# Four projection chunks of block one by seven block products, and another order of products in the first such chunk of block two

## The reference, cut to what matters

```python
hn = rms_norm(x, g_mix[l])
proj = hn @ w_in[l]
(qa, ka, va, ra, alr, qb, kb, vb, qi, ki, wi, gate_a, gate_b) = jnp.split(proj, split_points, axis=-1)
ya = gla_mixer(qa, ka, va, ra, alr, ...) @ w_br_gla[l]
yb = dsa_mixer(qb, kb, vb, qi, ki, wi, rel_bias) @ w_br_att[l]
mixed = jax.nn.sigmoid(gate_a) * ya + jax.nn.sigmoid(gate_b) * yb
x = x + mixed @ w_out[l]
x = x + hier_moe(rms_norm(x, g_ffn[l]), ...)
```

## Time and profile before

| | us |
|---|---|
| median of 3 runs | 933.66 (933.52 to 935.08) |
| the profiled execution, its own time | 934.74 |
| its span in the profile | 932.9 |

### The profile page before, as it was taken

The page is one execution under the profiler, slowest core; times in us unless marked ns, Lnnn a source line. Parts: engine busy times, 40 slices in busy tenths (PEclk is TensorE's granted clock), DMA queues, the critical chain, the costliest instruction groups (busy, mean ns, idle before and its releaser), DMA issues.

```text
span 932.9 us, 21571 instructions
## 1 busy us (share of the span) xinstructions
PE 792.4 (85%) x9619; PEld 578.7 (62%) x9619; DVE 260.1 (28%) x648; ACT 196.7 (21%) x415; POOL 71.1 (8%) x76
## 2 busy tenths in 40 slices
PE   7999999999999999999999888757676675756754
PEld 4565688884676657876757676646464464545643
DVE  2142930232422247684435111101001010010101
ACT  2112222331321133426525011101010020100100
POOL 6200300000001130190000000000000000000000
PEclk9999999999999999999999999988788899897988
DMA  9995624059899999444577999999999999999995
GB/s 304 329 330 183 245 93 179 1 197 420 325 396 416 402 364 331 162 174 163 225 268 298 422 430 424 426 427 427 427 428 431 429 430 428 428 429 427 428 428 229
DMA packets 55558, 310.18 MB, mean 332 GB/s; under 512 B 5426, under 2 KB 7178, under 8 KB 43088
## 3 DMA queue, kind: packets, MB, share of 16 engines
q1 hardware_dynamic: 50848, 301.60, 80.6%
q0 software_dynamic: 2912, 4.37, 1.6%
q10 hardware_dynamic: 1744, 3.41, 1.0%
HBM read 307.76 MB, written 4.19 MB: 334 GB/s over the span
## 4 chain that ended last, share of the span: by engine, by line
PE 62%; DMA 33%; issue 2%; DVE 2%; ACT 1%; DVEq 0%; SPq 0%; ACTq 0%
PE ps L1863 59%; DMA ring<-in_w_up 22%; DMA ring<-in_w_down 5%; DMA ring<-in_w_gate 5%; PE ps L1889 1%; PE ps L2191 1%; PE ps L2044 1%; DMA xx<-in_x 0%; PE ps L1903 0%; PE ps L2234 0%; PE ps L1920 0%; PE ps L2006 0%; ACT arena L845 0%; PE ps L2084 0%; PE ps L1911 0%
## 5 line engine op out<-in xcount | busy, mean ns | idle before, releaser
L1863 PE MATMUL ps<-ring,arena 128*32 128x128 f32 (+2 forms) x4912 | 228.9, 319 | 93.9 <-DMA ring<-in_w_gate 44.0
L1863 PEld LDWEIGHTS ps<-ring,arena 128*32 128x32 f32 (+1 forms) x4912 | 178.9, 126 | 142.6 <-DMA ring<-in_w_gate 52.8
L1863 PE MATMUL ps<-arena 32*128 32x256 f32 (+9 forms) x1412 | 143.3, 365 | 1.6 <-ACT arena L929 0.9
L1863 PEld LDWEIGHTS ps<-arena 32*128 32x128 f32 (+4 forms) x1412 | 96.3, 168 | 35.2 <-issue 27.9
L1863 PE MATMUL ps<-ring,xx 128*128 128x512 f32 (+2 forms) x344 | 114.4, 486 | 0.6 <-issue 0.6
L1863 PEld LDWEIGHTS ps<-ring,xx 128*128 128x128 f32 x344 | 64.2, 190 | 41.7 <-issue 34.9
L1863 PE MATMUL ps<-ring,const 128*32 128x256 f32 x864 | 58.8, 413 | 25.4 <-DMA ring<-in_w_down 22.4
L1863 PE MATMUL ps<-xx,ring 128*128 128x256 f32 x288 | 64.9, 382 | 0.0
L1863 PEld LDWEIGHTS ps<-ring,const 128*32 128x32 f32 x864 | 28.1, 116 | 52.2 <-issue 34.0
L1863 PEld LDWEIGHTS ps<-xx,ring 128*128 128x128 f32 x288 | 53.8, 190 | 8.0 <-issue 0.7
L918 ACT ACTIVATE g_dil<-ps 128x128 f32<-128x128 f32 x16 | 4.4, 277 | 189.0 <-PE ps L1863 189.0
(11 more groups left out here) (331 smaller groups left out, 713.0 us busy)
## 6 DMA issues: line engine op xcount, KB each, us to landing
ring<-in_w_up SPq DMA_DIRECT2D x37, 2048.0 KB, 25.1
ring<-in_w_gate SPq DMA_DIRECT2D x36, 2048.0 KB, 23.6
ring<-in_w_down SPq DMA_DIRECT2D x32, 2048.0 KB, 23.9
ring<-in_w_in SPq DMA_DIRECT2D x15, 2048.0 KB, 20.1
arena<-in_w_down SPq DMA_DIRECT2D x6, 2048.0 KB, 9.9
ring<-in_w_out SPq DMA_DIRECT2D x4, 2048.0 KB, 7.9
arena<-in_w_gate SPq DMA_DIRECT2D x4, 2048.0 KB, 16.0
arena<-in_w_up SPq DMA_DIRECT2D x2, 2048.0 KB, 17.4
```

Source lines behind the costliest of these rows:

```text
L1863: ins = pe.matmul(dst, w, x, start=start, stop=stop, skip_group_check=True)
```

## The change

- `chunk` and `tm_chunk` are replaced by one function `seven(c, s, q, block, between)` that does a chunk by seven products in an order given by `PRODUCTS[c]`. Chunks 0 to 3 are now kb, vb, va and ra of block one; the five of block two are chunks 4 to 8. `between` names what is done ahead of which product.
- The four chunks of block one share one pair of weight-sum buffers (at 80 of the arena) and their own buffers for the token sums (at 50). So the first weight sum of one chunk waits until the fourth product of the chunk before it is done. In block two there are two pairs, as before.
- ACT evicts five times in each of the four chunks (128 x 256), where it evicted once (128 x 512); DVE adds three times (128 x 256), where it evicted once, and makes four weight sums of 128 x 1024 each.
- The exponential of the GLA gate and its logarithm now stand inside the evictions of va, behind the transfer of the bias row, which stood behind them. The decays stand inside the evictions of ra. SiLU is no longer applied on the way out of PSUM: it is done in SBUF once all parts of ra are added.
- The second selection of DVE is cut in two: four rounds, then the addition and the weight sum of ra, then four rounds and the mask.
- In the first chunk of block two product 5 comes ahead of 6 and 3 ahead of 7; the forget logits move from behind product 1 to ahead of product 4 (the last), and ACT's absolute value and exponential of them, and what follows, into the next chunk. The forget sums move from between the second and third chunk into the third, ahead of product 7. DVE has the scale factors ahead of the second token sum.

```diff
-        t_sum = [[kb3(at + 4 * i, 4, T) for i in range(2)] for at in (62, 74)]
-        a_sum = [kb3(82 + 2 * i, 4, P) for i in range(4)]
+        t_sum = [[kb3(at + 4 * i, 4, T) for i in range(2)] for at in 4 * (80,) + (62, 74, 62, 74, 62)]
+        a_sum = [[kb3(at + 2 * i, 4, P) for i in range(4)] for at in (50, 82)]
...
-        SUM_BANKS = [(0, 1, 2), (3, 6, 7)]
+        SUM_BANKS = [(0, 1, 2), (3, 0, 1), (2, 3, 0), (1, 0, 3)] + 2 * [(0, 1, 2), (3, 6, 7)] + [(0, 1, 2)]
+        PRODUCTS = [(1, 2, 6, 5, 7, 3, 4)] * 4 + [(1, 2, 5, 6, 3, 7, 4)] + [(1, 2, 6, 5, 7, 3, 4)] * 4
...
+            chunk(0, k_tm, ahead=index_queries)
+            index_relu(0)
+            chunk(1, v_tm)
+            index_relu(1)
...
+            chunk(2, va, ahead=gate_exp, behind=gate_ln)
+            chunk(3, ra, behind=decays)
+            act.wait_ge(s_sev, 4 * N7 + 1)
+            act.wait_ge(s_pev_d, 7)
+            act.activation(ra, ra, ACT.Silu).then_inc(s_pev_a, 1)
...
                 if j == 1:
                     dve.wait_ge(s_slot[s % RING], turn_value(dve, 16 * (s // RING + 1), q, 16))
-                    if c >= 2:
+                    if 1 <= c < N7:
+                        dve.wait_ge(s_prod, 7 * (c - 1) + 4)
+                    elif c >= N7 + 2:
                         dve.wait_ge(s_prod, 7 * (c - 2) + 4)
...
-            select(1)
+            select(1, range(4))
+            add_second(ra, 3)
+            weight_sum(3, 4, 0)
+            select(1, range(4, TOPK // 8))
+            add_part(ra, 3)
+            add_third(ra, 3)
...
+            def seven(c, s, q, block, between={}):
+                arrived(s, q)
...
+                factors = {1: (bx, xnT[:, low, 0:P], w[:, low, left], True, False),
+                           2: (by, xnT[:, high, 0:P], w[:, high, left], True, True),
+                           3: (bz, s4, w[:, high, right], False, True),
+                           4: (bx, xnT[:, high, P:T], w[:, high, left], False, True),
+                           5: (bz, s1, t1, True, False),
+                           6: (bx, s2, t2, False, False),
+                           7: (bx, s3, w[:, low, right], False, False)}
+                for p in PRODUCTS[c]:
+                    b, x, w4, start, stop = factors[p]
+                    if p in between:
+                        between[p]()
+                    if p in (3, 4, 6, 7):
+                        pe.wait_ge(s_sev, act_out(c, {6: 1, 7: 6, 3: 5, 4: 7}[p]))
+                    if p in (3, 5, 6, 7):
+                        pe.wait_ge(s_asum, 4 * block + {5: 1, 6: 2, 7: 3, 3: 4}[p])
+                    if p in (4, 5, 6, 7):
+                        pe.wait_ge(s_tsum, 4 * c + {5: 1, 6: 2, 7: 3, 4: 4}[p])
+                    for k in range(4):
+                        ins = mm(bank(b, T), x[:, k, :], w4[:, k, :], start and k == 0, stop and k == 3)
+                    ins.then_inc(s_prod, 1)
...
+            seven(0, CH_KB, 0, 0, {1: lambda: evicted(1, 1), 6: index_transposes})
+            index_scores(0)
+            seven(1, CH_VB, 0, 0, {2: lambda: evicted(3, 3)})
+            index_scores(1)
...
+            seven(2, CH_VA, 0, 0, {5: lambda: evicted(5, 5)})
+            seven(3, CH_RA, 0, 0, {2: lambda: evicted(6, 6), 7: decay_sums})
...
+            block2_chunk(0, {5: lambda: pe.wait_ge(s_fpe, 1), 4: forget_logits})
+            block2_chunk(1)
+            block2_chunk(2, {7: forget_sums})
```

More of the change, by code:

```diff
@@ L891, in norm_by_tile, with out_of_psum, head_squares, chunk @@
                         act.dma_start(xs_dram[tt * P:(tt + 1) * P, :], xs[:, tt, :]).then_inc(s_xd, 16)
+            def out_of_psum(dst, c, p, b, tt):
+                act.wait_ge(s_prod, product_done(c, p))
+                if c < N7:
+                    return act.activation(dst, bank(b, T), ACT.Copy)
+                return act.activation(dst, bank(b, T), ACT.Copy, scale=x_rstd[:, tt:tt + 1])
+            def head_squares(x, i, evicted):
+                act.wait_ge(s_pev_a, CH_BG + evicted)
+                act.wait_ge(s_pev_d, 7 + evicted)
+                act.activation(kb(12 + 4 * i, 1024), x, ACT.Square).then_inc(s_sq, 1)
+            def chunk(c, dst, ahead=None, middle=None, behind=None):
+                bx, _, bz = SUM_BANKS[c]
+                out_of_psum(dst[:, 0, 0:T], c, 1, bx, 0).then_inc(s_sev, 1)
+                if ahead:
+                    ahead()
+                for p in ACT_OUTS[c][1:]:
+                    if p == 5:
+                        out_of_psum(c22_part[c], c, 5, bz, 1).then_inc(s_sev, 1)
+                    else:
+                        tt = int(p == 7)
+                        out_of_psum(dst[:, tt, T:2 * T], c, p, bx, tt).then_inc(s_sev, 1)
+                    if p == 6 and middle:
+                        middle()
+                if behind:
+                    behind()
+                last = out_of_psum(dst[:, 1, 0:T], c, 4, bx, 1)
+                last.then_inc(s_sev if c == 3 else s_pev_a, 1)
             def sparse_attention():
@@ L1043, in _ @@
             act.wait_ge(s_rs, FACTORS["x2"])
[L1045 to L1067, removed]
             def forget_abs_exp():
@@ L1612, in _ @@
             dve.tensor_scalar(q_tm[:, 1, :], bank(3), x_rstd[:, 1:2], None, ALU.mult).then_inc(s_pev_d, 1)
+            dve.wait_ge(s_xs, 2)
+            for j in range(1, 5):
+                x_sum(j, 0)
+            weight_sums(0, 0)
             dve.wait_ge(s_proj, 2)
@@ L1766, in _ @@
                                          op1=ALU.add).then_inc(s_fl, 1)
[L1767 to L1773 removed]
+            add_second(k2_tm, 5)
+            weight_sum(5, 4, q1)
+            weight_sums(6, q1)
             dve.wait_ge(s_fl, F_LN)
@@ L1951, in normed @@
                 pe.wait_ge((s_nev_a, s_nev_d)[k // 2 % 2], NEV0[m] + 2 * (k // 4) + k % 2 + 1)
-            def tm_chunk(w, b0, between=None):
-                for tt in range(TT):
-                    if tt == 1 and between:
-                        between()
-                    for k in range(KD):
-                        ins = mm(bank(b0 + tt), xnT[:, k, tt * P:(tt + 1) * P], w[:, k, :], k == 0, k == KD - 1)
-                ins.then_inc(s_proj, 1)
-                read[0] += 1
             def free_pair(n, base_a, base_d, last_d):
```

306 lines of the change are left out of this document (143 added, 163 removed).

## The result

| | before | after |
|---|---|---|
| median of six runs, us | 934.75 (933.52 to 937.64) | 929.69 (929.45 to 933.49) |
| ratio | | 0.9946, interval 0.9930 to 0.9962 |
| the profiled execution / its span | 934.74 / 932.9 | 933.49 / 931.7 |

The change makes the kernel 5.06 us faster. 7.0 was forecast, and the range ended at 929.6. Two things make up the distance between 926.7 and 929.69: the gain is 1.94 too small, and the kernel before, with three more runs, stands at 934.75 and not at 933.66, which is the other 1.09. The profiled execution of after happens to be its slowest, 3.8 above the median. TensorE also starts 0.68 later in it than in the kernel before.

What follows compares the result with a forecast made beforehand. It took TensorE's work up to about 500, then a fixed amount of bytes, as the bound. 7.4 - 2.3 + 1.9 = 7.0 off the median 933.66 gave 926.7, range 923.8 to 929.6.

Steps and rivals of the forecast that it cites:

- What bounds the kernel: Whole kernel: TensorE work up to about 500, then fixed bytes; a microsecond off TensorE before 500 moves the end by one.
- rival (e): Tail from slice 23 on moves fewer bytes a microsecond; gain gone from 1.6%, 936 at 2.2%; chance 0.04.
- Part 1: Block one's four chunks kb, vb, va, ra by seven products: 1.85 us saved in each, 7.4 off.
- rival (d): New waits for the chunks' evictions and sums, 0.35 for each of 20, eat the gain: 933.7; chance 0.05.
- Part 2: GLA behind ra: POOL's addition holds up DVE by the shared lock, so TensorE waits for `kdec`, 2.3 us back.
- rival (b): GLA: bias lands after 97.5, POOL's two additions run across `kdec`; wait 4.7, time 929.1; chance 0.12.
- Rival (a): GLA behind ra: no new wait, the lock between POOL and DVE is passed by; time 924.4; chance 0.16.
- Part 3: First chunk of block two: waits, 1.35 of them for ACT, go away; 1.9 us off, bounds 0.5 and 2.5.

## Why the prediction was wrong

- **What bounds the kernel: right.** What TensorE won ahead of 500 arrived at the end: 4.9 at the load for `xx`, 5.1 in the medians. The tail's rate is the same in the changed kernel (rival (e) is out for it), though with 32 one-element products a loss came there by another way.
- **Part 1, 7.4: the term was mis-sized; it is 6.51.** Two steps failed, this one (0.89) and the one that the prediction left out, told last (1.25). Here it took as the price of the old chunk less that of the new one 13.93 - 12.08 = 1.85, four times. It took 12.08 from the middle of a row of like chunks, from one start to another with products of the same kind on both sides, and 13.93 from a chunk that begins and ends beside other shapes. Like for like: va and the first tile of ra of before, 48 records, take 99.15 - 78.45 = 20.70 (view below), and the 16 of the second tile 107.87 - 100.83 = 7.04, so 32 in the middle cost 13.66 and the true difference there is 1.58; with both ends it is 1.64, as vb showed. Nothing of the 0.89 is a wait that the rows show: DVE's weight sums and ACT's evictions are hidden, as forecast, and rival (d) is out.

```profile
78.45 20.87 PE L1863 MATMUL ps<-ring,xx 128*128 128x512 f32 x48
...
100.83 7.11 PE L1863 MATMUL ps<-ring,xx 128*128 128x512 f32 x16
```

- **Part 2, 2.3 back: 1.91 (1.51 when run again); the mechanism is right, its timing was not, and that the sizes are near is luck.** The bias went out at 75.96, as worked out, but POOL could ask for it only at 90.17, 14.2 later, where it was 9.8 before (timelines of ACT and POOL below). It landed after 97.5, the case of rival (b); but (b) let both additions run behind each other across `kdec`. In fact `kdec` got in between them, and so waited for 2.1 us of the short one and not for 4.4 of the long. `add_part`, which I had held up, ran at 99.04 in 0.42. The late return I would put down to the two slot loads of 2 MB in the same stretch; that is argued, not tested. Rival (a) is out: the wait came.

```profile
75.96 0.61 ACTq L1064 DMA_DIRECT2D bias_scratch<-arena  x1
...
90.17 1.79 POOL L723 DMA_DIRECT2D arena<-bias_scratch  x2 [56.95 <-DMA bias_scratch<-arena]
```

- **Part 3, 1.9: 1.67.** ACT's wait of 1.35 is gone and one of 0.22 is left, at the last product.
- **Not in the sum at all: 1.25** in block one's experts, the largest miss. It is 1.10 of gaps where the program's pieces end and 0.15 of which no row tells. Adding instructions to TensorE's program moves the ends of its pieces. The prediction carried each microsecond won in block one unchanged up to 500, with nothing for this stretch and no reason for nothing.

Together 0.89 + 0.23 + 1.25 - 0.39 = 1.98, against 1.94. With the kernel before at its first median, the time would have been 928.6 and inside the range, so that the time came out just above it is partly chance: the range had nothing in it for the median of three runs being 1.1 low.

## What to carry to other kernels

Take the two prices that a term subtracts from the same kind of row, both with their ends or both without. When an engine's instructions are short and many, look at its idle times named "issue" before and after a change, and try a few harmless instructions where the engine waits anyway: here a piece's end inside such a run cost 0.3 to 1.3 us, and one placement, in which three turns of a loop were fetched again, made the tail 7 us longer. Look at the whole trace each time, since the filler can also change what comes long before or behind. Put an operation of POOL from SBUF to SBUF where nobody waits for DVE.

## What the hardware did that I had not expected

- TensorE stands still 0.3 to 1.3 us when a piece of its program ends inside a run of 31 ns instructions; behind 500, where weights are the bound, more idle times named "issue" stand (12 in the changed kernel, 13.6 us in all), and those cost nothing that was seen. With 32 products ahead, three turns of a loop were fetched again, nine fetches and some 6 us of standstill at the head of each; with 16 and with 48, a quarter of a piece either way, none was.
- A wait of 3.60 us was followed by a granted clock of 0.50 for over 4 us and cost 2.9 us on top of itself; waits of 1.3 and 1.72 at the same place cost nothing more.
- The granted clock was 0.79 from 80 to 95 us in one execution, and 0.68 from 75 to 80 in another, without an idle time just ahead of it.
